# Conformer convolution and sliding-window attention step: the order of GpSimd's weight remainders around the samples' convolution

## The reference, cut to what matters

```
z = u @ w_in;  a, b, gate = split(z, 3);  c = a * sigmoid(b)
full = concatenate([buf, c], axis=1)          # buf: the 30 inputs before
y = depthwise_conv(full, conv_w) + conv_b     # 31 taps, each feature for itself
out = (silu(layer_norm(y)) * silu(gate)) @ w_out
```

## Time and profile before

| | us |
|---|---|
| median of three runs | 3383.9 |
| span of the profiled execution | 3378.6 |
| TensorE matmul busy | 3197.5 (95%) |
| GpSimd busy | 1551.1 (46%) |
| VectorE busy | 1511.2 (45%) |
| ScalarE busy | 854.5 (25%) |

### The profile page before, as it was taken

One profiled execution on the slowest core, in us unless ns is written; L12 is line 12 of the kernel. 1 busy time (PEld: TensorE's weight loads), 2 busy tenths in 40 slices (PEclk: granted clock), 3 DMA queues, 4 the chain that ended last, 5 costly groups with the idle time before them and its releaser, 6 DMA issues.

```text
span 3378.6 us, 50475 instructions
## 1 busy us (share of the span) xinstructions
PE 3197.5 (95%) x19117; PEld 3077.4 (91%) x19117; DVE 1511.2 (45%) x1745; ACT 854.5 (25%) x1708; POOL 1551.1 (46%) x1153
## 2 busy tenths in 40 slices
PE   7999999999899999999778999999999999999995
PEld 6999999999899999999668998999899899899995
DVE  6999999999711131000560433244323343500043
ACT  5121121121222132212321322222222222332232
POOL 2777877878543324333353223332233223144475
PEclk9999999999899999999899999999999999899998
DMA  4122122122132252212453112111111211333386
GB/s 158 45 64 58 46 69 58 46 69 58 57 100 87 93 171 78 73 63 70 170 190 94 36 37 63 41 37 44 47 47 41 53 38 46 118 114 87 97 295 217
DMA packets 171677, 284.87 MB, mean 84 GB/s; under 512 B 62008, under 2 KB 72504, under 8 KB 171576
## 3 DMA queue, kind: packets, MB, share of 16 engines
q1 hardware_dynamic: 127328, 222.48, 22.2%
q10 hardware_dynamic: 41912, 52.32, 4.2%
q0 software_dynamic: 2352, 8.88, 0.7%
HBM read 218.44 MB, written 67.15 MB: 85 GB/s over the span
## 4 chain that ended last, share of the span: by engine, by line
PE 57%; POOL 17%; issue 12%; DVE 6%; DMA 4%; ACT 2%; SPq 1%; POOLq 0%; ACTq 0%; DVEq 0%
PE z_odd L512 9%; PE z_odd L513 8%; PE z_odd L515 8%; PE z_even L512 8%; PE z_even L513 7%; PE z_even L515 7%; POOL w_lo L1013 6%; POOL work L1094 4%; PE aux L609 3%; POOL work L1086 3%; PE z_even L627 2%; DMA work<-conv_scratch 1%; PE z_even L629 1%; POOL work L1122 1%; DMA work<-out_scratch 1%
## 5 line engine op out<-in xcount | busy, mean ns | idle before, releaser
L1013 POOL TENSOR_TENSOR w_lo<-w_raw,w_hi 128x512 fp32r<-128x512 f32 x528 | 746.7, 1423 | 1452.1 <-ACT w_hi L730 1451.6
L512 PE MATMUL z_even<-u_hi,w_hi 128*128 128x364 f32 (+1 forms) x2784 | 925.1, 332 | 80.7 <-POOL u_lo L1174 33.8
L512 PE MATMUL z_odd<-u_hi,w_hi 128*128 128x364 f32 (+1 forms) x2784 | 939.0, 337 | 58.9 <-POOL w_lo L1013 58.9
L513 PE MATMUL z_odd<-u_lo,w_hi 128*128 128x364 f32 (+1 forms) x2784 | 922.5, 331 | 0.0
L513 PE MATMUL z_even<-u_lo,w_hi 128*128 128x364 f32 (+1 forms) x2784 | 921.0, 331 | 0.0
L730 ACT ACTIVATE w_hi<-w_raw 128x512 fp32r<-128x512 f32 x528 | 331.4, 630 | 1730.5 <-PE z_even L515 810.3
L515 PE MATMUL z_odd<-u_hi,w_lo 128*128 128x364 f32 (+1 forms) x2784 | 636.5, 330 | 0.0
L515 PE MATMUL z_even<-u_hi,w_lo 128*128 128x364 f32 (+1 forms) x2784 | 635.3, 329 | 0.0
L512 PEld LDWEIGHTS z_even<-u_hi,w_hi 128*128 128x128 f32 x2784 | 529.8, 190 | 99.6 <-issue 30.7
L512 PEld LDWEIGHTS z_odd<-u_hi,w_hi 128*128 128x128 f32 x2784 | 531.7, 191 | 97.3 <-POOL w_lo L1013 55.1
L513 PEld LDWEIGHTS z_odd<-u_lo,w_hi 128*128 128x128 f32 x2784 | 532.1, 191 | 0.1
(11 more groups left out here) (148 smaller groups left out, 2405.1 us busy)
## 6 DMA issues: line engine op xcount, KB each, us to landing
w_raw<-in_w SPq DMA_DIRECT2D x528, 256.0 KB, 2.7
work<-in_x SPq DMA_DIRECT2D x32, 544.0 KB, 5.7
work<-branch_scratch SPq DMA_DIRECT2D x31, 544.0 KB, 5.5
conv_scratch<-work ACTq DMA_DIRECT2D x16, 544.0 KB, 2.7
work<-conv_scratch SPq DMA_DIRECT2D x16, 544.0 KB, 3.7
resid_scratch<-work ACTq DMA_DIRECT2D x16, 544.0 KB, 6.2
branch_scratch<-work ACTq DMA_DIRECT2D x16, 512.0 KB, 2.6
branch_scratch<-work POOLq DMA_DIRECT2D x15, 544.0 KB, 3.0
```

The lines of the kernel that those rows point to most:

```text
L512: pe.matmul(o, w_hi[:, q, at:at + P], chunk(u_hi[:, k, :], c), start=(i == 0), stop=False)
L513: pe.matmul(o, w_hi[:, q, at:at + P], chunk(u_lo[:, k, :], c), start=False, stop=False)
L1013: pool.tensor_tensor(w_lo[:, q, :], w_raw[:, q, :], w_hi[:, q, :].bitcast(F32), ALU.subtract).then_inc(w_lo_ready, 1)
```

## The change

GpSimd's order within `glu(j)`. Before: remainders q = 0 and q = 1 of tile 2j + 3, half 0, half 1, remainders q = 2 and q = 3. After: q = 0, half 0, q = 1 and q = 2, half 1, q = 3. Nothing else differs.

```diff
                 rest_w(2 * j + 3, 0)
-                rest_w(2 * j + 3, 1)
 
                 pool.wait_ge(z_read, 2 * j + 2)
...
                     if half == 0:
                         ins.then_inc(pool_step, 1)
+                        rest_w(2 * j + 3, 1)
+                        rest_w(2 * j + 3, 2)
                         pool.wait_ge(pool_step, at + 1)
                     else:
                         ins.then_inc(ys_ready, 1)
-                rest_w(2 * j + 3, 2)
                 rest_w(2 * j + 3, 3)
```

## The result

The changed kernel took 3362.48 us in the median of four runs (3357.08 to 3364.28), the kernel before 3382.52 (3379.92 to 3384.72, four runs with those shown). The ratio is 0.9937, with a 95% interval of 0.9923 to 0.9951: 0.6% faster. The profiled execution after took 3364.28 us with a span of 3362.6, so 1.7 us lie around the span, not 5.3.

A forecast was written before the change was run, and what follows sets the result against it. VectorE was taken to bound the convolution loop, through odd taps held up by GpSimd. 15.4 us from 14 turns plus 0.5 each from first and last gave -16.4: span 3362.2, with 5.3 around it 3367.5 us; range 3354 to 3378.

The forecast's parts named there:

- VectorE sets the turn, and the order acts through the odd taps' excess: Convolution loop: VectorE's 51.0 us turn is 42.4 us own work plus odd taps' time over 1.27 us, from GpSimd port contention.
- The walk: One loop turn traced tap by tap against GpSimd: excess 7.6 us instead of 8.95; 1.1 us a turn taken off.
- The size: Whole kernel: 15.4 us from 14 turns plus 0.5 us each from first and last, together -16.4 us.
- The first turn: Loop's first turn, where GpSimd is still paced by TensorE: 0.5 us saved.
- This one decides: Tap at 524.74 goes ahead of the line 1069 multiply; the next tap loses 1.13 us instead of 2.31.
- the two ties: Taps at 504.70 and 531.14 start almost with GpSimd instructions; GpSimd taken to win. Rival, VectorE wins: 3353 to 3358, 9%.
- the lower bound: Both near-simultaneous starts falling to VectorE: 6.5 us of excess, 2.2 off a turn, -31 us, 3353.
- TensorE's weights: Earlier remainders for TensorE's odd tile: the 3.5 us wait for q = 2 only changes place, value 0.
- The next weights 2.2 us later: Half 1 ends 2.2 us later, delaying history and weight loads and `w_hi`; ready as the multiply ends, value 0.
- that the multiply catches a tap again: Rival: line 1069's multiply is asked for ahead of a tap, +1.2 us a turn, no saving, 3384; 9%.
- the pair q = 1, 2 between the halves: Rival: these remainders cost taps at 512 to 516 1.1 us more, multiply still 2.3; slower, 3401; 7%.
- that TensorE was the bound: Rival: TensorE's 35.6 us of waiting for `w_lo` in the loop would vanish, 3348; 3%.

The follow-up runs named there:

- the pauses: One unused 128x32 GpSimd add per turn, in the old order ahead of the line 1069 multiply, in the new between q = 2 and half 1: 3364.3 and 3348.9 us.
- the PSUM runs: Odd taps take their second input from PSUM, leaving part of the result out, in the old and the new order: 3322.7 and 3325.0 us.
- before + pause: Old order plus one unused 128x32 GpSimd add ahead of the line 1069 multiply in each turn: 3364.3 us.
- before, multiply cut: Old order, with only the line 1069 GpSimd multiply cut into two of 544 elements: 3363.6 us.
- q = 1 alone: Against the kernel before, only remainder q = 1 moved from ahead of half 0 to between the halves: 3364.1 us.
- q = 2 alone: Against the kernel before, only remainder q = 2 moved from behind half 1 to between the halves: 3361.6 us.
- after, all cut: New order, with the loop's GpSimd remainders, two additions and multiply each cut into two of half length: 3323.9 us.
- before, all cut: Old order, with the loop's GpSimd remainders, two additions and multiply each cut into two of half length: 3340.4 us.

## Why the prediction was right, step by step

- *VectorE sets the turn, and the order acts through the odd taps' excess.* Right, and shown by the pauses (more work, less time) and by the PSUM runs (no excess, and TensorE sets the turn).
- *The walk.* Excess in the turn from 480.0, forecast and measured, from the third tap on: 0.49 and 0.48 (493.33), 0.52 and 0.51 (496.20), twice 0 and 0, 0.53 and 0.42 (503.87), 0.40 and 0.45 (508.01), 0.55 and 0.55, 0 and 0, 0.51 and 0.46, 1.13 and 1.11, 1.09 and 1.11. The turn was forecast at 49.9 and is 49.8 to 49.9 us, the multiply at 3.5 and is 3.52, the mean odd tap at 1.81 and is 1.793.
- *The size.* Forecast -16.4 us; the medians are 20.0 apart, the profiled spans 16.0. That the spans differ by just the forecast is luck. By line 1294's rows the 15 turns took 745.3 us in place of 764.6, 19.3 less, and the loop's last stretch 0.3 less. Fourteen turns gave 17.5 of that, 1.25 each where I had put 1.1, and the first gave 1.8 (47.9 after, 49.7 before), where I had put 0.5. Against this the first line 1294 stands 1.2 us later than before, and from TensorE's sum to the end are 2478.8 us in place of 2476.3; neither is touched by the change. What lies around the span was put at 5.3 us and is 1.7; the profiled execution of before, 3378.6 us of span, was simply one of its quicker ones.
- *The first turn.* The excess of its odd taps fell from 6.6 to 3.0 us, and VectorE then waited for TensorE in it (4.2 us and 0.7, in place of 2.9). That q = 1 no longer stands ahead of half 0 isn't needed for that: before + pause and before, multiply cut keep it there and have a first turn of 47.9 us too. Why the taps of before's first turn were held longer stays open.
- *"This one decides" said too much.* The step held in the kernel after. But q = 1 alone keeps the multiply's full hold and gains 1.0 us a turn through half 1. A turn has several places worth 0.5 to 1.2 us, and which of them pay is a matter of hundredths. The sum of the two ties was also taken too low for the lower bound: by the walk's own terms they are 0.52 and 1.09, 1.6 us a turn and not 1.1. It changed nothing, as neither fell to VectorE.
- *Ties.* I let the row at 505.32 decide them for GpSimd, and it was so again. In the kernel after, VectorE's and GpSimd's timelines read

```profile
496.20 1.78 DVE L1310 SCALAR_TENSOR_TENSOR work<-work,cols 128x1024 f32<-128x1024 f32 x1
...
496.22 0.68 POOL L1085 TENSOR_TENSOR work<-work,cols 128x248 f32<-128x248 f32 x1
```

  The tap came 0.02 us earlier and was held up all the same. The Trainium skill ("SBUF — State Buffer", SBUF: two separate sides) says that whichever of the two starts first gets the shared ports for its whole instruction; by the start times in these rows, that would have given this tap, forecast at 504.70, an excess of 0 in place of 0.51. The row chosen was a fair one: in the traces of the ten kernels whose odd taps read SBUF (94 to 855 us), a tap that starts less than 0.03 us ahead of GpSimd's next instruction is held (takes over 1.4 us) in 223 of 237 cases, one 0.03 to 0.06 us ahead in 64 of 171, and one 0.06 to 0.2 us ahead in none of 737. But the walks for q = 1 and q = 2 alone were off by 1.0 and 1.1 us a turn. A walk holds for one turn whose every request is a tenth of a microsecond from the next; where it isn't, its error is as large as the effect.
- *TensorE's weights.* Right that its wait would only change its place: 1.5 us for q = 1 and 0.2 for q = 3 in a turn, where I had put about 2, and 10.6 us in place of 5.5 at the end of the loop.
- *The next weights 2.2 us later.* They cost nothing, as forecast, but not quite for the reason given. The rounding starts at 519.75 and takes 0.63, to 520.38; the multiply ends at 520.31, so it no longer covers the rounding. The remainder at 520.46 would have had to wait for the tap at 519.02 all the same, which runs to 521.40, and that leaves 1.0 us of cover.

Of the rivals, that the multiply catches a tap again did not happen with the changed kernel and did with q = 1 alone; the pair q = 1, 2 between the halves cost the taps beside it 0.42 and 0.45 us and not 1.1 more; the ties went to GpSimd; and that TensorE was the bound is refuted by VectorE's rows, which hardly wait for it, and by both runs with a pause.

## What to carry to other kernels

Look at the durations of equal instructions on VectorE before looking at who waits for whom: a mean well above the shortest is time on the bounding engine that no wait shows. Where VectorE reads two inputs from SBUF beside a busy GpSimd, the length of GpSimd's single instructions can matter more than their number: here cutting them in two gained 42 us in the order of before and 39 in the order after, and a new order 20, by coincidences of less than 0.1 us. An order should be judged by runs, and only after the excess is gone does it show whether it serves the engine that waits.

## What the runs showed of the hardware

- A useless GpSimd instruction of 0.24 us made the kernel before 18 us and the kernel after 14 us faster.
- A GpSimd multiply of 2.51 us costs VectorE 2.3 us if it begins 0.01 us ahead of a tap (525.41 in the kernel before), and the next tap 1.1 if it is asked for during one and waits itself (516.79 in the kernel after).
- An odd tap whose second input is in PSUM takes 1.280 us in the mean, over 222 of them and none over 1.29, whatever GpSimd does beside it.
- GpSimd mostly goes on from one of its instructions to the next even when a tap's row starts up to 0.03 us earlier (505.32 and 505.35 in the kernel before; 223 of 237 cases), and never when the tap's starts 0.06 us earlier or more (737 cases); at 556.61 a tap 0.04 us ahead won.
- Cutting its long instructions is not free for GpSimd: with its waiting for VectorE included, it is busy 45.5 and 44.6 us in two turns of 47.6 (after, all cut), and 41.5 and 41.3 us in two of 49.9 in the kernel after. In the whole kernel its busy time rises from 1566.5 to 1624.7 us. The gain comes although it has more to do.
- TensorE's granted clock fell to 0.50 for 3.4 us towards the end of a stop of 3.6 us (before, all cut, idle from 843.9 to 847.46, clock down from 846.9), and matmuls then started 0.30 us apart in place of 0.17.
